# Gated stages of a four-part decoder trunk: weights stationary and tokens moving in units 1 to 10

## The chip, the cores and the metric

The kernel runs on one core of a Trainium2 chip, in one launch. The metric is the device time of one execution in microseconds. All arithmetic is single precision; the projections get it from the faster F32R format by splitting each operand into a high part and a low remainder and adding three products (high x high, high x low, low x high).

## The reference, cut to what matters

256 tokens of 1024 features go through six stages: gated (FF), short convolution, gated, gated, attention, gated. `F` is 2816. Every stage begins with an RMS norm. A gated stage is this:

```python
def rmsnorm(x, g):
    y = x32 * lax.rsqrt(jnp.mean(x32 * x32, axis=-1, keepdims=True) + RMS_EPS)
    return y.astype(x.dtype) * g

def swiglu(x, w_in, w_out):
    gate, up = jnp.split(x @ w_in, 2, axis=-1)      # w_in: 1024 x 5632
    return (jax.nn.silu(gate) * up) @ w_out         # w_out: 2816 x 1024

x = x + 0.5 * swiglu(rmsnorm(x, ln_ff1[i]), w_ff1_in[i], w_ff1_out[i])
```

The norm's factor (one number per token) is not applied to x. The transposed x carries only the gain, and the factor comes in after the projection.

## The kernel before, in words

Every engine has its own hand-written instruction stream; semaphores order them. `t` is one of two tiles of 128 tokens, `s` or `m` the stage, `u` a running count of input weight units, `o` one of output weight units, `c` one of hidden units, `j` the unit within a gated stage (0 to 10). Unit j of a gated stage covers 256 hidden features: 256 gate columns and 256 up columns of `w_in` stand side by side in a 512-column tile, with k = 0 to 7 over the 1024 inputs.

Weights. SP loads `raw_in` (four pieces) and `raw_out` (two halves). ACT copies them to `in_hi`, `out_hi` (`split_in`, `split_out`, lines 414 to 428), DVE subtracts to get `in_lo`, `out_lo` (lines 699 to 711). Both have two slots, used in turn; there is one `raw_in` and one `raw_out`, so SP's next load of a piece waits until DVE has split it.

TensorE. `project` (line 1063) has the transposed activations `xT_hi`, `xT_lo` of 128 tokens as the stationary operand and 512 weight columns as the moving one: 8 k x 3 matmuls for each t, into the bank `proj[t]`, tokens on partitions. ACT applies silu to the gate half of the bank, scaled by the norm factor `rstd` of each partition (`silu`, line 464). DVE multiplies it by the up half and `rstd` (`hidden`, line 766). TensorE transposes the 256 x 256 result in four 128x128 pieces into `tp[0]` (`transpose_hidden`, line 1128), ACT and DVE make `hT_hi` and `hT_lo` of it (lines 469 and 772), and `down_hidden` (line 1094) multiplies it by 256 rows of `w_out` into four `acc` banks that collect over the whole stage: 24 matmuls with 512 moving columns.

Order in a gated stage. `middle(j, par)` on each engine is one turn; TensorE's projects unit j and then does the down matmuls of unit j - 1. Unit 0 is projected first, unit 1 is `middle(1, 1)`, units 2 to 9 run in a loop of four turns with two units each, unit 10 is written out with the last down matmuls, `residual` (line 724: x plus acc times 0.5) and the next stage's norm. The projection of unit 1 waits piece by piece for its weights (`fresh`). An engine's queue is worked off in order, so a wait holds back what stands behind it.

Of the kernel before, what the change touches and what calls it, by code (L numbers as in the profile page):

```python
# [30 lines left out]
ALU = mybir.AluOpType  # L31
# [81 lines left out]
def build(nc, x_in, positions, ln_ff1, w_ff1_in, w_ff1_out, ln_mix, ln_ff2, w_ff2_in, w_ff2_out,  # L113
# [6 lines left out]
    with ExitStack() as ctx:  # L120
# [23 lines left out]
        ident = sb("ident", [P, P])  # L144
        band = sb("band", [P, 2 * P])
# [13 lines left out]
        rstd = sb("rstd", [P, 2 * 7])  # L159
        minus_half = sb("minus_half", [P, 1])  # L160
# [10 lines left out]
        hid_buf = gated[:, W:2 * W].rearrange("p (t n) -> p t n", t=NT)  # L171
        rope_cos = gated[:, 0:W]
# [57 lines left out]
        h_ready = sem("h_ready")  # L230
        hT_ps = sem("hT_ps")
# [133 lines left out]
        def _(pool):  # L365
# [6 lines left out]
            pool.wait_ge(consts_ready, 2)  # L372

# [24 lines left out]
            for m in range(len(STAGES) + 1):  # L398
                for t in range(NT):
# [6 lines left out]
                                       ALU.pow).then_inc(rstd_ready, 1)  # L406
                if m < len(STAGES) and STAGES[m] == ATTN:
                    for n in range(6):
                        rope_sums(n)
# [3 lines left out]
        def _(act):  # L413
# [45 lines left out]
            def silu(c, u, t, first_of=None):  # L459
                act.wait_ge(proj_done, 2 * u + t + 1)  # L460
                if first_of is not None:
                    act.wait_ge(rstd_ready, 2 * first_of + t + 1)
                    act.wait_ge(sq_ready, 2 * first_of + 2)
# [3 lines left out]
            def hidden_hi(c, slot):  # L467
                act.wait_ge(hT_ps, c + 1)
                act.activation(hT_hi[:, slot, :, :].rearrange("p k n -> p (k n)"), tp[0][:, :],  # L469
                               ACT.Copy).then_inc(hT_hi_done, 1)  # L470
# [14 lines left out]
            for s, kind in enumerate(STAGES):  # L485
# [3 lines left out]
                if kind == FF:  # L489
# [4 lines left out]
                    silu(c, u, 0, m)  # L494
                    split_in(u + 1, (u + 1) % 2, (2, 3))
                    silu(c, u, 1, m)
                    split_out(o, o % 2)
                    if s == 0:
# [17 lines left out]
                    silu(c + j, u + j, 0)  # L516
                    hidden_hi(c + j - 1, (c + j - 1) % 2)
                    split_out(o + j, (o + j) % 2)
                    if next_u:
                        split_in(next_u, next_u % 2, (0,))  # L520
                    silu(c + j, u + j, 1)
                    hidden_hi(c + j, (c + j) % 2)
                    if next_u:
                        split_in(next_u, next_u % 2, (1, 2, 3))
# [165 lines left out]
        def _(dve):  # L690
# [33 lines left out]
            def residual(m, t, scale):  # L724

                for half in range(2):
                    if t == 0:
# [5 lines left out]
                    part = x[:, t, half * W:(half + 1) * W]  # L733
                    dve.scalar_tensor_tensor(out=part, in0=acc[t][half][:, :], scalar=scale, in1=part,
# [26 lines left out]
            def hidden(c, t):  # L761

                dve.wait_ge(silu_done, 2 * c + t + 1)
                if not isinstance(c, int) or c >= 1:
                    dve.wait_ge(hT_ps, c)
                dve.scalar_tensor_tensor(out=hid_buf[:, t, :], in0=proj[t][:, UNIT:2 * UNIT],  # L766
                                         scalar=rstd_col[0][:, t:t + 1], in1=silu_buf[:, t, :],
                                         op0=ALU.mult, op1=ALU.mult).then_inc(h_ready, 1)

            def hidden_lo(c, slot):  # L770
                dve.wait_ge(hT_hi_done, c + 1)
                dve.tensor_tensor(hT_lo[:, slot, :, :].rearrange("p k n -> p (k n)"), tp[0][:, :],  # L772
                                  hT_hi[:, slot, :, :].rearrange("p k n -> p (k n)").bitcast(F32),
# [35 lines left out]
            for s, kind in enumerate(STAGES):  # L809
# [3 lines left out]
                if kind == FF:  # L813
                    c = NJ * FF_INDEX[s]
                    split_in(u + 1, (u + 1) % 2, (0, 1))
                    hidden(c, 0)
                    split_in(u + 1, (u + 1) % 2, (2, 3))
                    hidden(c, 1)
# [17 lines left out]
                    hidden(c + j, 0)  # L836
                    hidden_lo(c + j - 1, (c + j - 1) % 2)
                    split_out(o + j, (o + j) % 2)
                    if next_u:
                        split_in(next_u, next_u % 2, (0,))  # L840
                    hidden(c + j, 1)
                    hidden_lo(c + j, (c + j) % 2)
                    if next_u:
                        split_in(next_u, next_u % 2, (1, 2, 3))
# [557 lines left out]
```

## Time and profile before

| what | value |
|---|---|
| median of 3 runs | 956.91 us (955.53 to 957.76) |
| span of the profiled execution | 952.5 us |
| TensorE busy | 937.7 us, 98% |
| DVE, ACT busy | 542.6 us (57%), 440.6 us (46%) |
| weight loads (PEld) recorded | 774.3 us, 4363 of them |
| read from HBM | 167.31 MB, 177 GB/s over the span |

The page does not give the profiled execution a time of its own beside the span; the median of the runs is 4.4 us above the span. PE is the row of matmuls, PEld that of the loads of stationary operands, which overlap the matmuls. A matmul's recorded length (0.39 us) is longer than the distance to the next one's start, because matmuls are pipelined; throughput is read from starts. The granted clock is TensorE's share of its full 2.4 GHz.

### The profile page before, as it was taken

How to read it: one execution, taken by the hardware profiler on the slowest of the kernel's cores; microseconds unless marked ns; L12 is line 12 of the kernel's file. 1: busy time of each engine (PE TensorE's matmuls, PEld its weight loads, DVE VectorE, ACT ScalarE, POOL GpSimd, SP SyncE). 2: the span in 40 equal slices, each digit the busy share in tenths (PEclk: the TensorE clock that was granted, in tenths of full speed). 3: DMA queues.
4: the chain of work that ended last, by engine and by line, in shares of the span. 5: the costliest groups of instructions: out<-in, count | busy, mean ns of one | idle time of the engine just before them, and what ended most of it. 6: DMA issues, size and time to landing. Idle time of an engine off the chain costs nothing.

```text
span 952.5 us, 12737 instructions
## 1 busy us (share of the span) xinstructions
PE 937.7 (98%) x4363; PEld 774.3 (81%) x4363; DVE 542.6 (57%) x646; ACT 440.6 (46%) x615; POOL 28.2 (3%) x55
## 2 busy tenths in 40 slices
PE   7999999999999999999999999999999999999997
PEld 6888888888888888888888888888778888888885
DVE  5754554568656545545575454556866574554534
ACT  6553444456435534444354443534565473444432
POOL 1000000000000000000000000000411000000000
PEclk9999999999999999999999999999999999999999
DMA  8756474447644664656456566563440196465631
GB/s 277 255 186 212 147 223 158 155 154 266 221 146 156 189 216 150 213 166 201 145 197 205 180 198 199 162 218 106 156 154 16 48 318 215 151 215 164 199 109 44
DMA packets 122100, 168.81 MB, mean 177 GB/s; under 512 B 8589, under 2 KB 98773, under 8 KB 122069
## 3 DMA queue, kind: packets, MB, share of 16 engines
q1 hardware_dynamic: 121936, 168.35, 54.7%
q8 instruction: 20, 0.33, 0.1%
q14 instruction: 12, 0.09, 0.0%
q10 hardware_dynamic: 132, 0.04, 0.0%
HBM read 167.31 MB, written 1.05 MB: 177 GB/s over the span
## 4 chain that ended last, share of the span: by engine, by line
PE 94%; DVE 1%; DMA 1%; ACT 1%; POOL 1%; issue 1%; SPq 0%; ACTq 0%; DVEq 0%; POOLq 0%
PE acc L1090 30%; PE proj L1074 19%; PE proj L1076 19%; PE proj L1075 19%; PE tp L1134 2%; PE tp L1125 1%; PE tp L1140 1%; DMA raw_in<-in_w_ff_in 1%; PE proj L1272 1%; PE acc L1272 1%; POOL scratch L395 1%; PE acc L1298 1%; PE tp L1298 1%; DVE in_lo L703 0%; ACT gated L457 0%
## 5 line engine op out<-in xcount | busy, mean ns | idle before, releaser
L1074 PE MATMUL proj<-in_hi,xT_hi 128*128 128x512 f32 x848 | 336.9, 397 | 1.0 <-DVE xT_lo L758 0.6
L1076 PE MATMUL proj<-in_hi,xT_lo 128*128 128x512 f32 x848 | 331.4, 391 | 0.0
L1075 PE MATMUL proj<-in_lo,xT_hi 128*128 128x512 f32 x848 | 330.9, 390 | 0.0
L703 DVE TENSOR_TENSOR in_lo<-raw_in,in_hi 128x1024 fp32r<-128x1024 f32 x212 | 251.0, 1224 | 43.5 <-ACT in_hi L420 43.3
L420 ACT ACTIVATE in_hi<-raw_in 128x1024 fp32r<-128x1024 f32 x212 | 212.7, 1051 | 15.7 <-PE proj L1076 6.2
L464 ACT ACTIVATE gated<-proj,rstd 128x256 f32<-128x256 f32 x88 | 41.6, 473 | 363.7 <-PE proj L1076 363.7
L766 DVE SCALAR_TENSOR_TENSOR gated<-proj,rstd,gated 128x256 f32<-128x256 f32 x88 | 42.6, 484 | 274.5 <-ACT gated L464 274.3
L1074 PEld LDWEIGHTS proj<-in_hi,xT_hi 128*128 128x128 f32 x848 | 159.6, 188 | 35.2 <-issue 1.3
L1076 PEld LDWEIGHTS proj<-in_hi,xT_lo 128*128 128x128 f32 x848 | 159.6, 188 | 34.2
L1075 PEld LDWEIGHTS proj<-in_lo,xT_hi 128*128 128x128 f32 x848 | 159.9, 189 | 31.6
L710 DVE TENSOR_TENSOR out_lo<-raw_out,out_hi 128x1024 fp32r<-128x1024 f32 x96 | 114.2, 1230 | 6.1 <-ACT out_hi L428 6.1
L1090 PE MATMUL acc<-out_lo,hT_hi 128*128 128x512 f32 x352 | 110.1, 390 | 0.0
L1090 PE MATMUL acc<-out_hi,hT_hi 128*128 128x512 f32 x352 | 110.0, 390 | 0.0
L1090 PE MATMUL acc<-out_hi,hT_lo 128*128 128x512 f32 x352 | 109.1, 389 | 0.0
L428 ACT ACTIVATE out_hi<-raw_out 128x1024 fp32r<-128x1024 f32 x96 | 96.1, 1051 | 0.5 <-DMA raw_out<-in_conv_w_out 0.5
L1090 PEld LDWEIGHTS acc<-out_hi,hT_lo 128*128 128x128 f32 x352 | 66.1, 188 | 13.8
L1090 PEld LDWEIGHTS acc<-out_hi,hT_hi 128*128 128x128 f32 x352 | 66.1, 188 | 13.7
L1090 PEld LDWEIGHTS acc<-out_lo,hT_hi 128*128 128x128 f32 x352 | 65.8, 188 | 13.4
L772 DVE TENSOR_TENSOR hT_lo<-tp,hT_hi 128x512 fp32r<-128x512 f32 x44 | 30.4, 692 | 10.5 <-ACT hT_hi L469 7.6
L445 ACT ACTIVATE xT_hi<-pair 128x512 fp32r<-128x512 f32 x24 | 14.8, 633 | 46.8 <-DVE pair L749 46.8
L469 ACT ACTIVATE hT_hi<-tp 128x512 fp32r<-128x512 f32 x44 | 26.3, 598 | 7.1 <-PE tp L1134 7.1
L402 POOL TENSOR_SCALAR mean_sq<-sq_sum 128x1 f32<-128x1 f32 x14 | 2.7, 190 | 884.6 <-ACT gated L457 884.6
(102 smaller groups left out, 468.4 us busy)
## 6 DMA issues: line engine op xcount, KB each, us to landing
raw_in<-in_w_ff_in SPq DMA_DIRECT2D x352, 256.0 KB
raw_out<-in_w_ff_out SPq DMA_DIRECT2D x88, 512.0 KB, 5.4
raw_in<-in_conv_w_in SPq DMA_DIRECT2D x24, 512.0 KB
raw_in<-in_attn_w_qkv SPq DMA_DIRECT2D x12, 512.0 KB
raw_out<-in_conv_w_out SPq DMA_DIRECT2D x8, 512.0 KB, 5.4
raw_out<-in_attn_w_o SPq DMA_DIRECT2D x8, 512.0 KB, 3.3
x<-in_x SPq DMA_DIRECT2D x2, 512.0 KB, 4.6
scratch<-in_ln_final SPq DMA_DIRECT2D x1, 512.0 KB, 4.2
```

The source lines that it names most:

```text
L420: act.activation(in_hi[:, slot, 2 * q:2 * q + 2, :], raw_in[:, 2 * q:2 * q + 2, :], ACT.Copy).then_inc(in_hi_done, 1)
L428: act.activation(out_hi[:, slot, h, :], raw_out[:, h, :], ACT.Copy).then_inc(out_hi_done, 1)
L464: act.activation(silu_buf[:, t, :], proj[t][:, 0:UNIT], ACT.Silu, scale=rstd_col[0][:, t:t + 1]).then_inc(silu_done, 1)
L469: act.activation(hT_hi[:, slot, :, :].rearrange("p k n -> p (k n)"), tp[0][:, :], ACT.Copy).then_inc(hT_hi_done, 1)
L703: dve.tensor_tensor(in_lo[:, slot, 2 * q:2 * q + 2, :], raw_in[:, 2 * q:2 * q + 2, :], in_hi[:, slot, 2 * q:2 * q + 2, :].bitcast(F32), AL ...
L710: dve.tensor_tensor(out_lo[:, slot, h, :], raw_out[:, h, :], out_hi[:, slot, h, :].bitcast(F32), ALU.subtract).then_inc(out_lo_done, 1)
L766: dve.scalar_tensor_tensor(out=hid_buf[:, t, :], in0=proj[t][:, UNIT:2 * UNIT], scalar=rstd_col[0][:, t:t + 1], in1=silu_buf[:, t, :], op0 ...
L772: dve.tensor_tensor(hT_lo[:, slot, :, :].rearrange("p k n -> p (k n)"), tp[0][:, :], hT_hi[:, slot, :, :].rearrange("p k n -> p (k n)").bi ...
L1074: pe.matmul(proj[t][:, :], x_hi, in_hi[:, slot, k, :], start=(k == 0), stop=False)
L1075: pe.matmul(proj[t][:, :], x_hi, in_lo[:, slot, k, :], start=False, stop=False)
L1076: last = pe.matmul(proj[t][:, :], x_lo, in_hi[:, slot, k, :], start=False, stop=(k == KD - 1))
L1090: last = pe.matmul(acc[t][half][:, :], a, part, start=(start and n == 0), stop=(stop and n == 2))
```

## The change

In gated stages, units 1 to 10 exchange the operands of the projection. A 128-column block of the weights is the stationary operand and all 256 tokens are the moving one, so features stand on partitions and tokens along the row. `proj[0]` then holds the gate (two blocks of 256 tokens), `proj[1]` the up part. The product of silu and up is already in the form that the down matmuls take as `hT`, so units 1 to 10 have no transposes. Since the norm factor now varies along the row, it is made into a row: DVE scales the identity by `rstd` for each t, TensorE multiplies a matrix of ones by these diagonals, DVE copies the result, twice side by side, to `rstd_row`. DVE multiplies the gate by this row, ACT applies silu, DVE multiplies by the up part without the factor. Unit 0 keeps its old form but leaves the factor out of its up part too, and `residual` multiplies by `half_rstd` (0.5 times the factor, from POOL) where 0.5 stood. The diff, cut:

```diff
+            def project_f(u, slot, which, cs=(0, 1), fresh=False):
+                if not fresh:
+                    pe.wait_ge(in_lo_done, PIECES * (u + 1))
+                for c in cs:
+                    cols_of = slice((2 * which + c) * P, (2 * which + c + 1) * P)
+                    to = proj[which][:, c * SEQ:(c + 1) * SEQ]
+                    for k in range(KD):
+                        if fresh and c == 0 and k % 2 == 0:
+                            pe.wait_ge(in_lo_done, PIECES * u + k // 2 + 1)
+                        w_hi, w_lo = (a[:, slot, k, cols_of] for a in (in_hi, in_lo))
+                        pe.matmul(to, w_hi, xT_hi[:, k, :], start=(k == 0), stop=False)
+                        pe.matmul(to, w_hi, xT_lo[:, k, :], start=False, stop=False)
+                        last = pe.matmul(to, w_lo, xT_hi[:, k, :], start=False, stop=(k == KD - 1))
+                if 1 in cs:
+                    last.then_inc(proj_done, 1)
+            def row_of_rstd(f):
+                pe.wait_ge(diag_ready, 2 * f + 2)
+                for t in range(NT):
+                    last = pe.matmul(tp[1][:, t * P:(t + 1) * P], ones[:, :], rstd_diag[:, t * P:(t + 1) * P],
+                                     start=True, stop=True)
+                last.then_inc(rstd_row_ps, 1)
 # TensorE, stage body
-                    middle(1, 1, start=True)
+                    def middle(j, par):
+                        pe.wait_ge(gate_scaled, n0 + j)
+                        project_f(u + j, (u + par) % 2, 0)
+                        pe.wait_ge(hid_f_ready, n0 + j)
+                        project_f(u + j, (u + par) % 2, 1)
+                        down_before(j, par)
+                    pe.wait_ge(h_ready, 2 * f + 1)
+                    project_f(u + 1, (u + 1) % 2, 0, (0,), fresh=True)
+                    transpose_hidden(f, c)
+                    row_of_rstd(f)
+                    project_f(u + 1, (u + 1) % 2, 0, (1,))
+                    project_f(u + 1, (u + 1) % 2, 1)
+                    down_before(1, 1, start=True)
 # DVE
                     split_out(o, o % 2)
+                    rstd_to_row(f, m)
+                    hidden_lo(c, c % 2)
                     def middle(j, par):
-                        hidden(c + j, 0)
-                        hidden_lo(c + j - 1, (c + par + 1) % 2)
-                        split_in(u + j + 1, (u + par + 1) % 2, (0, 1, 2))
-                        hidden(c + j, 1)
-                        split_in(u + j + 1, (u + par + 1) % 2, (3,))
+                        split_in(u + j + 1, (u + par + 1) % 2, range(PIECES))
                         split_out(o + j, (o + par) % 2)
+                        gate_f_scaled(u + j, n0 + j)
+                        hidden_f(u + j, n0 + j)
+                        hidden_f_lo(c + j, (c + par) % 2)
+            def rstd_to_row(f, m):
+                for t in range(NT):
+                    dve.tensor_scalar(rstd_diag[:, t * P:(t + 1) * P], ident[:, :], rstd[:, 2 * m + t:2 * m + t + 1],
+                                      None, ALU.mult).then_inc(diag_ready, 1)
+                dve.wait_ge(rstd_row_ps, f + 1)
+                dve.tensor_copy(rstd_row.rearrange("p (k n) -> p k n", k=2),
+                                tp[1][:, 0:SEQ].unsqueeze(1).to_broadcast([P, 2, SEQ])).then_inc(rstd_row_ready, 1)
+            def gate_f_scaled(u, n):
+                dve.wait_ge(proj_done, 2 * u + 1)
+                dve.tensor_tensor(gate_f, proj[0][:, :], rstd_row, ALU.mult).then_inc(gate_scaled, 1)
+            def hidden_f(u, n):
+                dve.wait_ge(proj_done, 2 * u + 2)
+                dve.wait_ge(silu_f_done, n + 1)
+                dve.tensor_tensor(hid_f, proj[1][:, :], gate_f, ALU.mult).then_inc(hid_f_ready, 1)
 # ACT
                     def middle(j, par):
-                        silu(c + j, u + j, 0)
-                        hidden_hi(c + j - 1, (c + par + 1) % 2)
-                        split_in(u + j + 1, (u + par + 1) % 2, (0, 1, 2))
-                        silu(c + j, u + j, 1)
-                        split_in(u + j + 1, (u + par + 1) % 2, (3,))
+                        split_in(u + j + 1, (u + par + 1) % 2, range(PIECES))
                         split_out(o + j, (o + par) % 2)
+                        silu_f(n0 + j)
+                        hidden_f_hi(n0 + j, (c + par) % 2)
```

In unit 10 the order is the same on ACT and DVE with the next stage's first two pieces ahead of the silu and its last two behind the hidden value, and TensorE does 16 of the down matmuls of unit 9 before it waits for unit 10's hidden value.

## Rows read from the trace of the kernel before

**Rows 1.** The page: TensorE's busy time, share, instructions; the last chain, by engine.

```profile
PE 937.7 (98%) x4363; PEld 774.3 (81%) x4363; DVE 542.6 (57%) x646; ACT 440.6 (46%) x615; POOL 28.2 (3%) x55
...
PE 94%; DVE 1%; DMA 1%; ACT 1%; POOL 1%; issue 1%; SPq 0%; ACTq 0%; DVEq 0%; POOLq 0%
```

**Rows 2.** One middle unit, all engines; the first line names the columns.

```profile
core 0: us, PE busy (x) PEld busy (x) DVE busy (x) ACT busy (x) POOL busy (x), PEclk, DMA share, GB/s
307.48:324.29 16.81, 16.81 (x77) 13.91 (x76) 8.65 (x9) 7.20 (x9) 0.00 (x0) 1.00 0.77 244
```

**Rows 3.** The chain in order of time: start us, length us, what.

```profile
34.38 5.44 PE acc L1090 x24
```

**Rows 4.** TensorE around the transposes, by time: start us, length us, line.

```profile
307.25 0.39 PE L1076 MATMUL proj<-in_hi,xT_lo 128*128 128x512 f32 x1
307.49 0.60 PE L1134 MATMUL tp<-ident,gated 128*128 128x128 f32 x4
307.84 0.48 PE L1074 MATMUL proj<-in_hi,xT_hi 128*128 128x512 f32 x1
308.15 0.40 PE L1075 MATMUL proj<-in_lo,xT_hi 128*128 128x512 f32 x1
308.39 0.40 PE L1076 MATMUL proj<-in_hi,xT_lo 128*128 128x512 f32 x1
...
310.47 0.39 PE L1076 MATMUL proj<-in_hi,xT_lo 128*128 128x512 f32 x1
```

**Rows 5.** Weight loads in order of time, same stretch.

```profile
307.81 0.19 PEld L1074 LDWEIGHTS proj<-in_hi,xT_hi 128*128 128x128 f32 x1
307.92 0.19 PEld L1075 LDWEIGHTS proj<-in_lo,xT_hi 128*128 128x128 f32 x1
```

**Rows 6.** Weight loads of 64-column matmuls; each row begins with a start.

```profile
702.64 0.30 PEld L1298 LDWEIGHTS acc<-scratch 128*128 128x128 f32 x2
...
702.75 0.30 PEld L1298 LDWEIGHTS acc<-scratch 128*128 128x128 f32 x2
```

**Rows 7.** TensorE at the lower clock: one window, then two starts.

```profile
684.10:687.30 3.20, 3.20 (x10) 2.52 (x9) 3.04 (x4) 2.49 (x3) 1.38 (x2) 0.50 0.01 3
...
685.46 0.63 PE L1074 MATMUL proj<-in_hi,xT_hi 128*128 128x512 f32 x1
685.89 0.63 PE L1075 MATMUL proj<-in_lo,xT_hi 128*128 128x512 f32 x1
```

**Rows 8.** Score matmuls, 256 columns; each row begins with a start.

```profile
700.30 0.59 PE L1272 MATMUL acc<-scratch 64*128 64x256 f32 x2
...
700.51 0.59 PE L1272 MATMUL acc<-scratch 64*128 64x256 f32 x2
...
700.73 0.38 PE L1272 MATMUL acc<-scratch 64*128 64x256 f32 x1
```

**Rows 9.** Second gated stage: TensorE, ACT, DVE after unit 0's projection.

```profile
302.04 0.39 PE L1074 MATMUL proj<-in_hi,xT_hi 128*128 128x512 f32 x1
...
302.24 0.47 ACT L464 ACTIVATE gated<-proj,rstd 128x256 f32<-128x256 f32 x1 [1.49 <-PE proj L1076]
...
302.75 0.48 DVE L766 SCALAR_TENSOR_TENSOR gated<-proj,rstd,gated 128x256 f32<-128x256 f32 x1
303.70 2.36 DVE L710 TENSOR_TENSOR out_lo<-raw_out,out_hi 128x1024 fp32r<-128x1024 f32 x2 [0.47 <-ACT out_hi L428]
```

**Rows 10.** The last gated stage at the same place.

```profile
771.08 0.50 PE L1074 MATMUL proj<-in_hi,xT_hi 128*128 128x512 f32 x1
...
772.63 1.22 DVE L703 TENSOR_TENSOR in_lo<-raw_in,in_hi 128x1024 fp32r<-128x1024 f32 x1
...
774.16 2.35 DVE L710 TENSOR_TENSOR out_lo<-raw_out,out_hi 128x1024 fp32r<-128x1024 f32 x2
```

**Rows 11.** Groups by line: busy us, mean ns of one, idle time before.

```profile
L772 DVE TENSOR_TENSOR hT_lo<-tp,hT_hi 128x512 fp32r<-128x512 f32 x44 | 30.4, 692 | 10.5 <-ACT hT_hi L469 7.6
...
L866 DVE TENSOR_SCALAR scratch<-scratch,cols 128x256 f32<-128x256 f32 x8 | 2.3, 349 | 1.4 <-ACT scratch L540 1.4
```

More of the change, by code:

```diff
@@ L144, in build @@
         ident = sb("ident", [P, P])
+        ones = sb("ones", [P, P])
         band = sb("band", [P, 2 * P])
@@ L171, in build @@
         hid_buf = gated[:, W:2 * W].rearrange("p (t n) -> p t n", t=NT)
+        gate_f, hid_f = gated[:, 0:W], gated[:, W:2 * W]
+        rstd_row = pair[:, 0, :]
+        rstd_diag = pair[:, 1, 0:SEQ]
         rope_cos = gated[:, 0:W]
@@ L230, in build @@
         h_ready = sem("h_ready")
+        half_ready = sem("half_ready")
+        diag_ready = sem("diag_ready")
+        rstd_row_ps = sem("rstd_row_ps")
+        rstd_row_ready = sem("rstd_row_ready")
+        gate_scaled = sem("gate_scaled")
+        silu_f_done = sem("silu_f_done")
+        hid_f_ready = sem("hid_f_ready")
         hT_ps = sem("hT_ps")
@@ L372, in _ @@
             pool.wait_ge(consts_ready, 2)
+            pool.memset(ones[:, :], 1.0).then_inc(ident_ready, 1)
             pool.affine_select(out=band[:, :], in_=band[:, :], compare_op=ALU.is_ge, fill=NEG, base=-1,
@@ L406, in _ @@
                                        ALU.pow).then_inc(rstd_ready, 1)
+                    if m < len(STAGES) and STAGES[m] == FF:
+                        pool.wait_ge(rstd_ready, i + 1)
+                        pool.tensor_scalar(half_rstd[:, i:i + 1], rstd[:, i:i + 1], 0.5, None,
+                                           ALU.mult).then_inc(half_ready, 1)
                 if m < len(STAGES) and STAGES[m] == ATTN:
@@ L493, in _ @@
                     split_in(u + 1, (u + 1) % 2, (0, 1))
-                    silu(c, u, 0, m)
+                    silu(u, 0, m)
                     split_in(u + 1, (u + 1) % 2, (2, 3))
-                    silu(c, u, 1, m)
+                    silu(u, 1, m)
                     split_out(o, o % 2)
+                    f = FF_INDEX[s]
+                    n0 = (NJ - 1) * f - 1
+                    hidden_hi(f, c % 2)
                     if s == 0:
@@ L722, in split_late_out, with residual @@
                                       ALU.subtract).then_inc(out_lo_done, 1)
-            def residual(m, t, scale):
+            def residual(m, t):
                 for half in range(2):
+                    if t == 0 and half == 0 and STAGES[m - 1] == FF:
+                        dve.wait_ge(half_ready, 2 * (FF_INDEX[m - 1] + 1))
                     if t == 0:
@@ L733, in residual @@
                     part = x[:, t, half * W:(half + 1) * W]
+                    i = 2 * (m - 1) + t
+                    scale = half_rstd[:, i:i + 1] if STAGES[m - 1] == FF else 1.0
                     dve.scalar_tensor_tensor(out=part, in0=acc[t][half][:, :], scalar=scale, in1=part,
@@ L759, in norm_rest, with hidden @@
                                       xT_hi[:, ks, ts].bitcast(F32), ALU.subtract).then_inc(xT_lo_done, 1)
[L761 to L768, printed above, removed]
+            def hidden(f, t):
+                dve.wait_ge(silu_done, 2 * f + t + 1)
+                if f >= 1:
+                    dve.wait_ge(hT_ps, f)
+                dve.tensor_tensor(hid_buf[:, t, :], proj[t][:, UNIT:2 * UNIT], silu_buf[:, t, :],
+                                  ALU.mult).then_inc(h_ready, 1)
             def hidden_lo(c, slot):
@@ L1046, in _ @@
                 for t in range(NT):
-                    residual(m + 1, t, 0.5 if kind == FF else 1.0)
+                    residual(m + 1, t)
                     if s + 1 < len(STAGES):
@@ L1163, in _, with down_before @@
                     c = NJ * FF_INDEX[s]
-                    def middle(j, par, start=False):
-                        for t in range(NT):
-                            pe.wait_ge(h_ready, 2 * (c + j - 1) + t + 1)
-                            project(m, u + j, t, (u + par) % 2, fresh=(start and t == 0))
-                            if t == 0:
-                                transpose_hidden(c + j - 1)
+                    f = FF_INDEX[s]
+                    n0 = (NJ - 1) * f - 1
+                    def down_before(j, par, start=False):
                         pe.wait_ge(hT_lo_done, c + j)
@@ L1183, in _ @@
                     j = NJ - 1
-                    for t in range(NT):
-                        pe.wait_ge(h_ready, 2 * (c + j - 1) + t + 1)
-                        project(m, u + j, t, (u + j) % 2)
-                        if t == 0:
-                            transpose_hidden(c + j - 1)
+                    pe.wait_ge(gate_scaled, n0 + j)
+                    project_f(u + j, (u + j) % 2, 0)
+                    pe.wait_ge(hid_f_ready, n0 + j)
+                    project_f(u + j, (u + j) % 2, 1)
                     pe.wait_ge(hT_lo_done, c + j)
@@ L1192, in _ @@
                     slots = ((c + j - 1) % 2, (o + j - 1) % 2)
-                    down_hidden(*before, 0, *slots, parts=range(0, 4))
-                    transpose_hidden(c + j)
-                    down_hidden(*before, 0, *slots, parts=range(4, 6))
+                    down_hidden(*before, 0, *slots)
                     down_hidden(*before, 1, *slots, parts=range(0, 2))
```

60 lines of the change are left out of this document (36 added, 24 removed).

## Prediction

> **What bounds the kernel now.** I read the page first, then the windows of single units, then single starts on TensorE. The page shows TensorE busy for 98% of the span, and the chain of waits that ended last lies on it for 94% [rows 1]. So the time is a count of matmuls times the distance between their starts. One middle unit of a gated stage takes 16.81 us; TensorE fills all of it at the full granted clock (1.00, which is 2.4 GHz), while DVE works 8.65 us and ACT 7.20 us in it and the DMA engines are 0.77 busy [rows 2]. Nothing but TensorE ends a wait there. Its 24 matmuls of the down projection take 5.44 us, 0.2267 us each [rows 3]. A unit has 48 + 24 such matmuls, 16.32 us; the other 0.49 us of 16.81 belong to the four transposes. They are seen in the starts: last matmul before them at 307.25, transposes from 307.49, the second matmul after them at 308.15, and the ten distances from there to 310.47 mean 0.232 us and not 0.227 [rows 4].
>
> The number that decides is not in a busy share: how long TensorE needs from start to start when the moving operand is 256 columns and every matmul has a new stationary tile. Loads and streams overlap: a load begins just as the matmul before it does, and in a run of 512 columns it is out of sight [rows 4, 5].
>
> **The change, part by part.**
>
> *1. The projections of units 1 to 10.* Out go 48 matmuls of 512 columns per unit, in come 96 of 256 columns (two outputs, two column blocks, eight k, three products). The columns streamed are the same, the weight loads double. There are 40 such units. The bounds of one 256-column distance:
> - A load occupies its port for about 0.11 us: two loads after a pause start at 307.81 and 307.92 [rows 5], and in a run of 64-column matmuls the loads set the beat at 0.11 us (702.64, 702.75) [rows 6]. So 0.112 us is the floor, an estimate from these starts.
> - The stream: 512 columns at 2.4 GHz are 0.2133 us, the measured distance is 0.2267, so 0.0133 us are lost per matmul. If the loss goes with the columns, 256 cost 0.1133 us. If it goes with the load or with the instruction, they cost 0.1067 + 0.0133 = 0.120 us.
> - Which? At the lower granted clock (0.50, 1.2 GHz) the distance is 0.427 us, exactly 512 columns with nothing lost [rows 7]. So the loss is not a fixed count of array cycles; it is something on the supply side that does not show when the array is slow. The plain F32 score matmuls, 256 columns streamed twice, stand 0.21 and 0.22 us apart [rows 8], again with nearly nothing lost, though each has a load. And after a pause the distance wanders (0.23 to 0.24 us) before it settles [rows 4]. A loss that depends on how load and stream stand to each other looks like the two disturbing each other, and then each load costs it. In the new loop a load runs beside almost all of each stream, so I take 0.120 us. The widest distance there, 0.24 us from 308.15 to 308.39, is a loss of 0.0267 us and bounds it above: 0.1067 + 0.0267 = 0.133 us. Below: 0.112.
> Sum: 96 x 0.120 + 24 x 0.2267 = 11.52 + 5.44 = 16.96 us per unit without transposes, against 16.81 with them: +0.15 us, times 40 = **+6 us**. At the ends of the range: 0.112 gives 16.19, -0.62 us, -25 us in all; 0.133 gives 18.21, +1.40 us, +56 us in all. Each 0.001 us in this distance is 3.8 us in the result.
>
> *2. The transposes.* Eleven groups of four per stage become one (unit 0 keeps its own). That is the 0.49 us of each of 40 units, 19.6 us, and it is already inside the +6 (the projections alone cost +25.6).
>
> *3. The norm factor as a row, once per stage.* DVE scales two 128x128 diagonals (some 0.25 us each, an estimate from 349 ns for 128x256 [rows 11]), TensorE multiplies them by ones (two plain F32 matmuls, which the kernel's others show as two records each, so four at the load's 0.11 us), DVE copies the row. TensorE's part of it is about 0.45 us, and 0.1 us for the load that shows after a wait. But the diagonals stand on DVE behind the two splits of the down weights, and TensorE waits for them in order, with 72 projection matmuls queued behind. In the stage at 302 us unit 0's last projection ends at 302.04; silu follows at 302.24, the hidden product at 302.75, the splits of the down weights on DVE run from 303.70 to 306.06 [rows 9]. The diagonals would be ready at about 306.6. TensorE has 24 short matmuls (2.9 us) and the transposes (0.44 us) to fill the time: it is there at 305.4 and waits 1.3 us. In the stage at 771 us (and in the first stage, which is built and fed alike) the weights of unit 1 arrive late: TensorE starts at 771.08, the last piece of unit 1 is split at 773.85, the down weights at 776.51 [rows 10]. Now the first half covers 2.9 us and not 5.4: about 0.55 us of waiting for the last piece, transposes until 775.1, diagonals at 777.1, 2.0 us of waiting. Sum: 2 x 1.3 + 2 x 2.55 + 4 x 0.6 = **+10 us**. This could be nothing if the splits came later than the diagonals, which the order forbids; at worst the splits wait for a transfer, another 1 us per stage.
>
> *4. DVE and ACT in a middle unit.* DVE loses two products of 0.48 us [rows 9] and one of 692 ns and gets three 512-column operations of about 692 ns [rows 11]: 8.65 - 1.66 + 2.07 = 9.1 us of some 17. ACT stays at about 7 us. The splits now run in one block from the end of a unit's projections: some 2.5 us for the hidden value, then 6 pieces at 1.22 us on DVE, over about 10 us later, and the gate of the next unit is ready 11 us later. What waits behind it: the product with the row must be done before TensorE needs that bank again, some 10 us later. Cost nothing; the cover is the 5.4 us of down matmuls and 5.8 us of the other half of the projection, and each microsecond beyond it would be 40 in the result. SP's loads follow the same splits, which come in one block and have about 9 us to land. At a share of 0.77 [rows 2] the bytes of a unit keep the DMA engines 12.9 us busy, so they fit in 17 us; cost nothing, with the same 40 for each microsecond of lateness.
>
> *5. Small edits, one answer.* The residual takes its factor from a column that POOL made a stage earlier, and hidden rows leave one factor out: same instruction, no cost. The extra fill of ones is done on POOL before x has arrived. At a stage's end the last hidden value is ready 2.4 us after its projection, and 16 down matmuls (3.6 us) cover that, where four transposes stood before.
>
> **The sum.** Span 952.5 + 6 + 10 = 968.5 us. The median of the runs, 956.9, is 4.4 above the profiled span; with the same 4.4 the forecast is 973 us.
>
> **The rivals.**
> - *A, the loss goes with the columns or vanishes (faster).* The distance is then 0.112 to 0.1145 us. At 0.1133 the projections cost what they did, the transposes give 19.6 back, the boundaries take 10: 947 us. For it: rows 8, where streams with loads lose nearly nothing. Against: rows 4, where the distance changes with the same columns. It decides below 0.1158 us, where 3840 x 0.0025 equals the 9.6 us that are left.
> The Trainium skill has a rule that ends on this side: "TensorE: Matmul & The Clock Gate", Back-to-back issue gap, gives columns / 2.4 + 2.5 ns for a warm stream, 109 ns for 256 columns; worked out from the page, an estimate, the sum is 931 us. For 512 columns it gives 216 ns, and the trace has 227 [rows 3]; the measurement decides.
> - *B, nearly even.* 0.1145 to 0.117 us: 952 to 961 us.
> - *C, load and stream disturb each other more when both last 0.107 us.* 0.124 to 0.133 us: 988 to 1023 us. For it: every stream is now under a load from end to end. Against: a steady run settles at the smallest loss [rows 4].
> - *D, loads don't hide.* Each load is recorded with 0.19 us [rows 5]. If that were its real occupancy, 96 x 0.188 + 5.44 = 23.5 us per unit, +267 us, some 1235 us. Against: loads that start 0.11 us apart [rows 5, 6].
> A page speaks for D: "Perfetto Trace Analysis" in the Trainium skill, Identifying the Most-Contended Engine, takes the busy share of LDWEIGHTS as the measure of TensorE's headroom; it is 13.91 of 16.81 us here [rows 2], and the change adds 48 loads to 76.
>
> **How the numbers follow.** The forecast (0.117 to 0.124 us, 961 to 988 us): 0.51. A: 0.22. B: 0.07. C: 0.16. D: 0.04. About 0.2% is what a measurement of this kernel can tell from no change. Faster: A and a little of B, 0.24; same, 955 to 959: 0.04; slower 0.72. The range reaches from A's 944 to 1004 us (0.128), in the middle of C; it leaves out D, the upper half of C and the lowest edge of A. The likeliest case's own range is 961 to 988.
>
> **What would show it.** In the changed profile: the down matmuls still 0.2267 us apart; the new projection matmuls in a steady run 0.120 apart (0.113 says A, over 0.124 says C, 0.19 or more D); a unit of 16.96 us; TensorE idle 1.3 to 2.6 us once per gated stage, ended by DVE's diagonal; no idle time in the loops. The prediction is wrong if the distance is off by more than 0.003 us, or if the loops show waits for DVE, ACT or a transfer.

## The result, and the profile after

| | before | after |
|---|---|---|
| median of the runs | 956.2 us (955.5 to 957.8, 4 runs) | 972.65 us (970.2 to 975.3, 4 runs) |
| span of the profiled execution | 952.5 us | 970.3 us |
| TensorE matmul records | 4363 | 6139 |

The change makes the kernel slower: the ratio is 1.0181, with a 95% interval of 1.0162 to 1.0200. The forecast was 973. One execution of ten of the kernel "High and low x side by side" below took 1559 us at a mean granted clock of 0.557 and is left out of its numbers; all others in this document had 0.98 or more.

The page of the changed kernel, busy time by engine and the chain by engine, beside [rows 1]:

```profile
PE 948.5 (98%) x6139; PEld 860.9 (89%) x6139; DVE 559.5 (58%) x658; ACT 436.3 (45%) x575; POOL 34.5 (4%) x64
...
PE 90%; DVE 3%; DMA 2%; ACT 2%; POOL 1%; issue 1%; SPq 1%; DVEq 0%; POOLq 0%; ACTq 0%
```

TensorE is as full as before, and the weight loads rise from 81% to 89% busy. The chain leaves TensorE more often than before (90% and not 94%).

One middle unit, from the end of one block of down matmuls to the end of the next, beside [rows 2]:

```profile
core 0: us, PE busy (x) PEld busy (x) DVE busy (x) ACT busy (x) POOL busy (x), PEclk, DMA share, GB/s
326.74:343.72 16.98, 16.98 (x122) 16.02 (x122) 9.88 (x11) 7.79 (x9) 0.00 (x0) 1.00 0.58 194
```

And the same unit's neighbours in the chain in order of time (start us, length us, what), beside [rows 3]:

```profile
321.27 5.47 PE acc L1147 x24
338.25 5.47 PE acc L1147 x24
```

A unit takes 338.25 - 321.27 = 16.98 us, where it was 16.81; TensorE still has no gap in it. (In the kernel before the units alternate between 16.81 and 16.79 us, so their mean is 16.80; the changed kernel's are all 16.98.) The new projection matmuls, TensorE by time:

```profile
350.03 0.28 PE L1197 MATMUL proj<-xT_hi,in_hi 128*128 128x256 f32 x1
350.15 0.28 PE L1198 MATMUL proj<-xT_lo,in_hi 128*128 128x256 f32 x1
350.27 0.28 PE L1199 MATMUL proj<-xT_hi,in_lo 128*128 128x256 f32 x1
```

Each row's length (0.28 us) is how long one matmul is in the engine; what it costs is the distance to the next start, 0.12 us.

The second gated stage at its boundary, all engines by time, to be read against [rows 9]:

```profile
308.17 0.42 DVE L795 TENSOR_TENSOR gated<-proj,gated 128x256 f32<-128x256 f32 x1 [0.18 <-ACT gated L480]
...
309.12 2.36 DVE L735 TENSOR_TENSOR out_lo<-raw_out,out_hi 128x1024 fp32r<-128x1024 f32 x2 [0.52 <-ACT out_hi L445]
...
310.34 0.60 PE L1217 MATMUL tp<-ident,gated 128*128 128x128 f32 x4
...
311.40 0.48 DVE L807 TENSOR_SCALAR pair<-ident,rstd 128x128 f32<-128x128 f32 x2
...
311.93 0.71 PE L1207 MATMUL tp<-pair,ones 128*128 128x128 f32 x4 [0.99 <-DVE pair L807]
312.39 0.36 PE L1197 MATMUL proj<-xT_hi,in_hi 128*128 128x256 f32 x1
```

DVE's hidden product and splits are at 308.17 and 309.12, TensorE's transposes at 310.34, and TensorE then waits for the two diagonals, which DVE makes behind the splits of the down weights. Over the whole kernel, the waits of the weight loads:

```profile
PEld tp L1207 <- DVE pair L807: 6.1, 4, 1.8
```

Four waits, one in each gated stage, 6.1 us in all. Where the 17.8 us of span went can be read from the transposes of x that open each stage; in the chain of the changed kernel those of five stages are

```profile
199.31 0.87 PE tp L1182 x8
...
292.21 0.87 PE tp L1182 x8
...
482.28 0.87 PE tp L1182 x8
...
672.35 0.87 PE tp L1182 x8
...
768.91 0.88 PE tp L1182 x8
```

and in the chain of the kernel before they stand at

```profile
194.25 0.87 PE tp L1125 x8
...
286.79 0.87 PE tp L1125 x8
...
473.45 0.87 PE tp L1125 x8
...
660.10 0.87 PE tp L1125 x8
...
755.61 0.87 PE tp L1125 x8
```

So the first gated stage takes 199.31 - 194.25 = 5.1 us more than before, the convolution stage 0.4, the second and third gated stage 3.4 each, the attention stage 1.1, and the last gated stage (to the end of the span) 4.5. In the convolution and attention stages TensorE has the same matmuls in every kernel of this document, and yet they take 92.5 to 93.0 us and 93.9 to 97.3 us in its ten traces. So their 0.4 and 1.1 us are within what varies from trace to trace, and the change itself costs the 16.4 us of the four gated stages, which is also the difference of the two medians.

### The profile page after: what moved, and what is told of

Its sections match the earlier page's. It is cut to its first block, busy times and chain, and to the rows that moved or that the text cites. A ratio compares the mean times of both kernels' runs of the same rounds, so it can differ in the third digit from the quotient of the medians.

```text
span 970.3 us, 16110 instructions
## 1 busy us (share of the span) xinstructions
PE 948.5 (98%) x6139; PEld 860.9 (89%) x6139; DVE 559.5 (58%) x658; ACT 436.3 (45%) x575; POOL 34.5 (4%) x64
## 4 chain that ended last, share of the span: by engine, by line
PE 90%; DVE 3%; DMA 2%; ACT 2%; POOL 1%; issue 1%; SPq 1%; DVEq 0%; POOLq 0%; ACTq 0%
PE acc L1147 28%; PE proj L1199 15%; PE proj L1198 15%; PE proj L1197 15%; PE proj L1131 4%; PE proj L1133 4%; PE proj L1132 4%; DMA raw_in<-in_w_ff_in 1%; DVE out_lo L735 1%; PE tp L1223 1%; PE tp L1182 1%; DVE in_lo L728 1%; PE proj L1363 1%; PE acc L1363 1%; POOL scratch L408 1%
## 5 line engine op out<-in xcount | busy, mean ns | idle before, releaser
L1197 PE MATMUL proj<-xT_hi,in_hi 128*128 128x256 f32 x1280 | 363.0, 284 | 1.3 <-DVE gated L795 0.9
L1199 PE MATMUL proj<-xT_hi,in_lo 128*128 128x256 f32 x1280 | 362.2, 283 | 0.0
L1198 PE MATMUL proj<-xT_lo,in_hi 128*128 128x256 f32 x1280 | 362.2, 283 | 0.0
L1197 PEld LDWEIGHTS proj<-xT_hi,in_hi 128*128 128x128 f32 x1280 | 245.5, 192 | 4.4 <-DVE gated L795 1.7
L1198 PEld LDWEIGHTS proj<-xT_lo,in_hi 128*128 128x128 f32 x1280 | 245.6, 192 | 1.5
L1199 PEld LDWEIGHTS proj<-xT_hi,in_lo 128*128 128x128 f32 x1280 | 245.5, 192 | 0.0
L823 DVE TENSOR_TENSOR gated<-proj,gated 128x512 f32<-128x512 f32 x40 | 27.7, 692 | 184.4 <-PE proj L1199 181.3
L735 DVE TENSOR_TENSOR out_lo<-raw_out,out_hi 128x1024 fp32r<-128x1024 f32 x96 | 113.1, 1219 | 24.4 <-ACT out_hi L445 24.4
L1131 PE MATMUL proj<-in_hi,xT_hi 128*128 128x512 f32 x208 | 83.6, 402 | 1.0 <-DVE xT_lo L787 1.0
L1133 PE MATMUL proj<-in_hi,xT_lo 128*128 128x512 f32 x208 | 81.5, 392 | 0.0
L1132 PE MATMUL proj<-in_lo,xT_hi 128*128 128x512 f32 x208 | 81.5, 392 | 0.0
```

Source lines behind the costliest of these rows:

```text
L735: dve.tensor_tensor(out_lo[:, slot, h, :], raw_out[:, h, :], out_hi[:, slot, h, :].bitcast(F32), ALU.subtract).then_inc(out_lo_done, 1)
L823: dve.tensor_tensor(hid_f, proj[1][:, :], gate_f, ALU.mult).then_inc(hid_f_ready, 1)
L1131: pe.matmul(proj[t][:, :], x_hi, in_hi[:, slot, k, :], start=(k == 0), stop=False)
L1132: pe.matmul(proj[t][:, :], x_hi, in_lo[:, slot, k, :], start=False, stop=False)
L1133: last = pe.matmul(proj[t][:, :], x_lo, in_hi[:, slot, k, :], start=False, stop=(k == KD - 1))
L1197: pe.matmul(to, w_hi, xT_hi[:, k, :], start=(k == 0), stop=False)
```

## The experiments

**Diagonals first.** The changed kernel, with the two diagonals made by DVE ahead of the splits of the down weights.

```diff
                     hidden(f, 1)
+                    rstd_diagonals(f, m)
                     split_out(o, o % 2)
                     rstd_to_row(f, m)
```

> The changed kernel, with the two diagonal scalings on DVE moved ahead of the two splits of the down weights (the copy of the row stays behind them). Theory: TensorE's four waits for the diagonal (1.85, 1.27, 1.27 and 1.85 us from the last transpose to the next record, 5.8 us over the usual distance) vanish and nothing is late next, because the copy of the row is needed only 10 us later: 5.8 us less than the changed kernel, about 966.8 us. Rival: unit 1's hidden value or its weights are late next and the wait only moves: under 1 us gained, 972 us.

Measured: 963.5 us (962.9 to 966.3, 4 runs), ratio to the kernel before 1.0081 (1.0057 to 1.0106). The changed kernel's ratio is 1.0181, so this one edit gives back about 1.0% of the time by the medians, 0.6% by the profiled spans (970.3 - 964.5 = 5.8 us; the gated stages alone are 6.2 us shorter). The forecast of this run was 966.8; the profiled execution, 966.3 us, was the slowest of the four and the other three took about 963. Where those 3 us come from isn't shown. TensorE around the boundary of the second gated stage, by time:

```profile
308.08 0.60 PE L1221 MATMUL tp<-ident,gated 128*128 128x128 f32 x4
308.51 0.61 PE L1211 MATMUL tp<-pair,ones 128*128 128x128 f32 x4
308.88 0.36 PE L1201 MATMUL proj<-xT_hi,in_hi 128*128 128x256 f32 x1
```

The row of the norm factor follows the transposes at once. From transposes to next projection it is 0.80 us and not 2.05 (312.39 - 310.34). The order on DVE was the cause of the wait, and no other work of DVE took its place here. One new gap of 0.6 us is in this trace, at 41 us, before unit 2 of the first stage, and ends with DVE's gate product; the last kernel below is without it.

**The kernel before with 256 columns.** Only the length is changed: tokens stay stationary, each projection of units 1 to 10 is done in two blocks of 256 weight columns, the transposes stay.

```diff
+                wide = W // parts
+                for part in range(parts):
+                    cs = slice(part * wide, (part + 1) * wide)
...
-                    pe.matmul(proj[t][:, :], x_hi, in_hi[:, slot, k, :], start=(k == 0), stop=False)
+                        pe.matmul(proj[t][:, cs], x_hi, in_hi[:, slot, k, cs], start=(k == 0), stop=False)
```

> The kernel before, in which only the projections of units 1 to 10 of each gated stage are cut into two column halves: same operands and roles, tokens stationary, 96 matmuls of 256 columns where 48 of 512 stood; transposes and all waits as before. Theory (the loss of 13.3 ns is paid per matmul, whatever its operands): distance 0.120 us, 1920 more matmuls x 0.0133 = +25.6 us over the kernel before, about 982 us. Rival (the loss goes with the exchange of roles, for example because weights that DVE has just written are now loaded as stationary tiles): distance 0.1133 us, no change, 956 us.

Measured: 977.9 us (977.5 to 979.8), ratio 1.0241 (1.0214 to 1.0268), span 975.6. A window of one unit, with the columns of [rows 2], and TensorE by time:

```profile
353.29:370.70 17.41, 17.41 (x126) 16.45 (x125) 8.65 (x10) 7.19 (x10) 0.00 (x0) 1.00 0.57 182
```

```profile
350.09 0.28 PE L1078 MATMUL proj<-in_lo,xT_hi 128*128 128x256 f32 x1
350.21 0.28 PE L1079 MATMUL proj<-in_hi,xT_lo 128*128 128x256 f32 x1
```

The distance is 0.12 us with the other operand stationary and other data. It belongs to the length, not to the exchange of the operands. The unit is 17.41 us, 0.60 over the kernel before; the changed kernel's is 16.98, and the 0.43 us between them are the transposes.

The time is 4 us under the 982 that was expected. The units give 24.4 us and not 25.6, since the 0.06 us that the transposes disturb behind them in the kernel before are not there at 256 columns (96 x 0.120 + 24 down matmuls in 5.47 + four transposes in 0.43 are 17.42 us). The attention stage is 1.6 us shorter in this trace (93.9 and not 95.5 us): it has no stretch at the lower clock, where the kernel before has 3.4 us of it.

**The transposes twice.** The kernel before, with each group of four transposes of the hidden value done two times over.

```diff
-                for kt in range(2):
+                for kt in (0, 1, 0, 1):
```

> The kernel before, with each group of four transposes of the hidden value done twice into the same places. Theory: TensorE has no slack, so 44 groups x 4 x 0.108 us = +19.1 us, about 975 us. Together with the unit's 16.81 us this gives the price of a group, 0.49 us, of which 0.06 us stay with the change of pattern. Rival: part of the transposes runs in time that TensorE has anyway: less than +12 us.

Measured: 973.65 us (973.0 to 975.4), ratio 1.0194 (1.0167 to 1.0221), span 971.6, +19.1 in span. The down matmuls of two units in a row in its chain:

```profile
34.81 5.44 PE acc L1090 x24
52.06 5.44 PE acc L1090 x24
```

The unit is 17.25 us here, +0.44 (17.23 and +0.43 in the mean of two). That is the difference between the last two kernels again, to 0.01: the second group costs the bare four transposes, and the 0.06 us of disturbed matmuls behind a group come once. Of the 19.1 us 0.8 are the attention stage's (last section); the gated stages' 18.4, over the 44 groups of the kernel, are 0.42 each.

**The vector engine does more.** The changed kernel, with DVE's product for the hidden value done once more into a buffer that nobody reads.

```diff
+                dve.tensor_tensor(rstd_twin, proj[1][:, :], gate_f, ALU.mult)
                 dve.tensor_tensor(hid_f, proj[1][:, :], gate_f, ALU.mult).then_inc(hid_f_ready, 1)
```

> The changed kernel, with the product of the up part and the activated gate made once more on the vector engine, into a buffer that nobody reads: 0.69 us more on that engine in each of 40 units, just ahead of the hidden value that the down projection waits for. Theory (there is slack of several us behind the 48 products of the other half): no change, ratio to the changed kernel 0.999 to 1.001, so about 972.5 us. Rival (the vector engine's chain is already close to the limit in a unit): up to 40 x 0.69 = 28 us more, 1000 us.

Measured: 970.8 us (970.6 to 971.7, 4 runs), ratio to the kernel before 1.0161 (1.0142 to 1.0180), so not slower than the changed kernel. Its chain:

```profile
37.74 5.47 PE acc L1149 x24
54.72 5.47 PE acc L1149 x24
```

A unit stays at 16.98 us. 40 x 0.68 = 27 us more work on DVE costs nothing; DVE is no bound in the changed loop.

**Half the stationary columns.** The kernel before, with 64 of the 128 token columns as stationary operand in the projections of units 1 to 10; half the tokens' projection is left out there. It asks where the 0.0133 us beyond the stream come from.

```diff
-                    x_hi, x_lo = (a[:, k, t * P:(t + 1) * P] for a in (xT_hi, xT_lo))
+                    x_hi, x_lo = (a[:, k, t * P:t * P + rows_of] for a in (xT_hi, xT_lo))
```

> The kernel before, with only 64 of the 128 token columns of the stationary operand in the projections of units 1 to 10; the projection of half the tokens is left out there. 48 x 40 matmuls of 512 columns keep their stream and get a load of half as many columns. Theory 1 (the 13.3 ns over the stream are what the array needs between two matmuls, whatever is loaded): distance 0.2267 us as before, time unchanged, ratio 0.998 to 1.002. Theory 2 (the load takes something from the stream while it runs, in proportion to its size): distance 0.220 us, 1920 x 0.0067 = 13 us less, about 942 us, ratio 0.986. Theory 3 (the loss is in the number of rows that a matmul writes): the same 0.220 us, which this run does not tell from theory 2.

Measured: 962.1 us (959.8 to 963.4), ratio 1.0073 (1.0054 to 1.0092), a unit of 16.95 us: no theory expected slower. Loads by form, then starts on TensorE by time:

```profile
L1075 PEld LDWEIGHTS proj<-in_lo,xT_hi 128*64 128x64 f32 x640 | 86.2, 135 | 56.3
...
L1075 PEld LDWEIGHTS proj<-in_lo,xT_hi 128*128 128x128 f32 x208 | 39.1, 188 | 7.5
```

```profile
357.09 0.40 PE L1075 MATMUL proj<-in_lo,xT_hi 128*64 128x512 f32 x1
357.33 0.39 PE L1076 MATMUL proj<-in_hi,xT_lo 128*64 128x512 f32 x1
...
359.17 0.39 PE L1075 MATMUL proj<-in_lo,xT_hi 128*64 128x512 f32 x1
```

The load is recorded shorter (135 ns and not 188), but the distance grows: nine distances from 357.09 to 359.17 mean 0.231 us and not 0.227, and they vary from row to row. So the loss is not in proportion to the size of the load. Beyond that its cause stays open.

**128 columns.** The kernel before with four blocks of 128 columns, the edit as above with `parts=4`.

> The kernel before, with the projections of units 1 to 10 cut into four blocks of 128 columns: 192 matmuls with their weight loads per unit in place of 48, the same columns and the same products. A stream of 128 columns takes 0.053 us, so the load is the longer of the two. Theory (a load occupies its port for about 0.11 us and hides all else): distance 0.107 to 0.112 us, unit 192 x 0.11 + 5.44 + 0.49 = 27.0 us, +10.2 us x 40, about 1365 us. Rival 1 (the 13 ns come on top of the longer of the two): 0.122 us, unit 29.4 us, about 1455 us. Rival 2 (13 ns on top of the stream, loads always hidden): 0.067 us, about 1020 us.

Measured: 1393 us (one execution), span 1391.4. TensorE by time, a pair of units in the chain, and a window near the start with its granted clock:

```profile
129.99 0.28 PE L1077 MATMUL proj<-in_hi,xT_hi 128*128 128x128 f32 x1
130.10 0.27 PE L1078 MATMUL proj<-in_lo,xT_hi 128*128 128x128 f32 x1
130.21 0.28 PE L1079 MATMUL proj<-in_hi,xT_lo 128*128 128x128 f32 x1
```

```profile
119.68 5.50 PE acc L1093 x24
146.98 5.50 PE acc L1093 x24
```

```profile
26.00:66.00 40.00, 40.00 (x183) 39.42 (x183) 10.87 (x22) 7.07 (x12) 0.00 (x0) 0.50 0.29 93
```

The distance is 0.11 us, where the stream alone would be 0.053: with 128 columns the load sets the beat, as forecast from [rows 5, 6]. The unit is 27.3 us, 40 x 10.5 = 420 us of the 439 us of span. The first gated stage takes 20 us more than that, and they are in the window: from 26 to 66 us the granted clock was 0.50 (1.2 GHz); there the short matmuls stand 0.213 us apart. They began at 22.65 us, and TensorE paused twice before the clock fell: ahead of 24.34 and of 25.47 us, the second time for 0.25 us for a piece of the weights. I had not foreseen that, and one execution doesn't show its cause.

**High and low x side by side.** "Diagonals first", and then the one use of the exchange that makes instructions longer: the high part of the weights is multiplied by [high x | low x], 512 columns, and the low part by high x, 256 columns into the second half of the same bank; DVE adds the halves. That is 32 + 32 matmuls per unit in place of 96.

```diff
-                        pe.matmul(to, w_hi, xT_hi[:, k, :], start=(k == 0), stop=False)
-                        pe.matmul(to, w_hi, xT_lo[:, k, :], start=False, stop=False)
-                        last = pe.matmul(to, w_lo, xT_hi[:, k, :], start=False, stop=(k == KD - 1))
+                        pe.matmul(both, in_hi[:, slot, k, cols_of], xT[:, :, k, :], start=(k == 0), stop=False)
+                    for k in range(KD):
+                        last = pe.matmul(to[:, SEQ:2 * SEQ], in_lo[:, slot, k, cols_of], xT_hi[:, k, :],
+                                         start=False, stop=(k == KD - 1))
```

> The kernel with early diagonals, in which the two products that share a weight tile (high weights by high x and by low x) become one matmul of 512 columns, high x and low x side by side, and the low weights' product adds into the second half; the two halves are added by DVE (ten more 256-column operations in the place of two of 512, less two), and the up part uses the two tp banks. Theory (a fixed 13.3 ns per matmul): per block and k 0.2267 + 0.120 = 0.3467 us in the place of 0.360, 32 of them per unit: 0.43 us less per unit, 17 us less than the kernel with early diagonals: about 950 us, 6 below the kernel before. Rival: the mixture of lengths never settles (5 ns more per 512-column matmul, 6 us) or the longer DVE chain (about 1.7 us more from the end of a projection to the hidden value) shows at the stage ends, 1 us each: 956 to 960 us.

Measured: 953.6 us (951.7 to 955.8), ratio 0.9981 (0.9965 to 0.9997), span 951.8. Its chain, and its waits on TensorE:

```profile
54.41 5.47 PE acc L1163 x24
71.03 5.47 PE acc L1163 x24
```

```profile
PE proj L1213 <- DVE in_lo L730: 1.9, 4, 0.6
PE proj L1213 <- DVE gated L827: 1.2, 1, 1.2
```

The unit is down to 16.62 us, where 16.55 (0.43 less than 16.98) had been expected: 40 x 0.19 = 7.6 us won in the loop against the kernel before. Most of it went into waits outside it: for late pieces in the first units (line 730), and 1.2 us at 41 us for the gate, which DVE makes behind the rotary angles in the first stage.

**The same, with those waits cured.** Unit 1 takes the wide and the narrow product of each k in turn, all others 16 wide and then 16 narrow ones; the rotary angles come after unit 1's hidden value.

```diff
-                    for k in range(KD):
-                        if fresh and c == 0 and k % 2 == 0:
...
+                if fresh:
+                    for k in range(KD):
...
+                        wide(0, k)
+                        last = narrow(0, k)
```

> The kernel of the run before with 512-column products for the high weights, cured of the waits that its trace showed: in the first half of unit 1 the 512-column product and the 256-column product of one k follow each other, so that a late piece of the weights blocks less; in all other units both column blocks of a half run their 16 wide products first and then their 16 narrow ones, so that the length changes once and not twice per half; the angles of the rotary table are computed after unit 1's hidden value and not before it. Theory (TensorE's starts alone set the time): the wait of 1.58 us at 41 us goes, the waits for late pieces shrink from 3.5 us in all to about 2.3, and half of the changes of length go, 80 times some 0.02 us. Span 951.8 - 1.6 - 1.2 - 1.6 = 947.4 us, time about 949, ratio to the kernel before 0.993 to 0.994. Rival (the late pieces are set by the transfers, the angles then delay the loop instead): 952 to 954 us, ratio 0.997 to 1.000.

Measured: 950.5 us (948.5 to 951.8, 6 runs), ratio 0.9942 (0.9926 to 0.9958), span 950.0. The waits and the chain:

```profile
PE proj L1211 <- DVE gated L797: 0.6, 1, 0.6
```

```profile
52.16 5.47 PE acc L1163 x24
68.73 5.47 PE acc L1163 x24
```

The wait for the gate at 41 us is gone (line 827 no longer stands among TensorE's waits), the late pieces cost 0.3 us and not 1.9, and the unit is 16.57 us. The three edits were made together, so what each gave was not taken apart. This kernel beats both: 0.6% faster than the one before, 2.3% faster than the changed one (950.5 / 972.65). By the spans it is 2.5 us under the kernel before; its gated stages alone are 4.8 us shorter, and its attention stage, 1.8 us longer in this trace, hides the rest.

## Why the prediction was right

The forecast was right in its time and, nearly everywhere, in its working. Two errors of about 2 us nearly cancel: the span is 970.3 and not 968.5 us, and the median is 2.3 and not 4.4 us above it. They are largely one error. Each execution on record takes 1.8 to 1.9 us longer than its own span, so some 2.5 of the 4.4 us were only that the profiled execution of the kernel before was quicker than its median one. From median to median the forecast added 16 us, and 16.4 were measured. That it hit 973 to 0.4 us is luck all the same: the four executions of the changed kernel lie 5 us apart.

- *Step 1, the distance.* 0.120 us was taken of bounds 0.112 to 0.133, and 0.120 it is, in both kernels that were tried with 256 columns. The choice between "the loss goes with the columns" and "the loss goes with the instruction" carried the sign of the answer; A's 0.1133 would have made the change a gain. The unit is 16.98 us and not 16.96, since the 24 down matmuls take 5.47 us and not 5.44: the first few behind a change of length are up to 0.01 us late. That is +7 us in 40 units where 6 were forecast. The reason given, that load and stream disturb each other, is not shown: the loss is there once per matmul, but half a load did not lower it. Every projection matmul in these kernels has a load of its own, so no run tells a loss per load from a loss per instruction. The plain F32 score matmuls of [rows 8] show nearly none of it, and no run asked why. So the distance was right, and its reason stays open.
  What hangs on rival A's page follows: by the rule in the Trainium skill, "TensorE: Matmul & The Clock Gate", Back-to-back issue gap, 256 columns would stand 109 ns apart; the trace has 120 ns, and 227 for 512 columns where the rule gives 216. The section gives this rule for the gap of a single matmul, without a budget for loads, which the prediction did not say. The measurement decides.
- *Step 2, the transposes.* 0.49 us was taken; the two pairs of kernels give 0.43 us for the four transposes themselves, and 0.06 for what they disturb behind them. It was already inside the unit.
- *Step 3, the boundaries.* In the middle stages 10 x 0.15 + 1.3 + 0.6 = 3.4 us was forecast, and both measured 3.4. In detail: the wait is 1.2 us and not 1.3, the ten units 1.8 and not 1.5, and 0.4 us and not 0.6 are left for the rest. The waits in the first and the last stage are 1.8 us and not 2.0. In the first and the last stage 4.65 us was forecast and 5.1 and 4.5 measured. "Diagonals first" shows that it is this wait: without it the span is 5.8 us shorter, where 2 x 1.3 + 2 x 2.0 = 6.6 had been put down for the diagonals. What then stays at each boundary beside the units (row matmuls, late pieces) is 0.4 us in the middle stages, 0.9 in the last and 1.3 in the first, 0.6 of it the new gap at 41 us.
- *Step 4, the other engines.* No cost, and none found: the units show no gap, and 0.69 us more of DVE in each changed nothing. DVE was put at 9.1 us, and the nine instructions of a unit add up to that: 3 x 0.69 for the products and the low part, 4.63 for the splits of four pieces, 2.35 for those of two halves, 9.05 in all. The window shows 9.88 because a part of the next unit's instructions falls into it. The gate's product of that unit starts at 332.53, and TensorE takes its bank again at 343.56, 10.3 us after the product has ended.
- *Step 5, small edits.* The end of a stage shows 36 down matmuls in a row and the transposes of x behind them: nothing waits for the last hidden value there.
- *Not forecast.* The convolution stage takes 0.4 us more and the attention stage 1.1, which were put at nothing; these 1.5 us are most of the error in the span, and they vary as much between traces of other kernels. That the offset of one execution to the median carries over was an assumption, and it was off by 2 us.
- *Rival D* falls: the loads are recorded with 0.19 us and stand 0.12 apart, with 89% of the span busy. By the Trainium skill, "Perfetto Trace Analysis", Identifying the Most-Contended Engine, TensorE's headroom is judged by the busy share of LDWEIGHTS, together with the share of peak FLOPs that is used; by the share of the loads alone, as the prediction took it, [rows 2] leaves 2.9 us of 16.81, room for 15 loads of 0.19 us, and the trace has 44 more in a unit that grew by 0.17 us. The overlap of the records decides here, not their share.

## What to carry to other kernels

Cost a matmul by the distance of starts at its own moving length, from the trace: here, at 512 and at 256 columns, a fixed 0.013 us sits on each F32R matmul with its load beside 0.1067 us per 256 columns. So twice the instructions for the same columns cost 24 us in 40 units, more than the 17 us that the saved transposes gave. If an exchange of the operands puts two products on the same stationary tile, join them into one long stream, which is where the gain was. And ahead of a serial step that TensorE waits for, look at what stands in front of it on its engine: two 0.28 us scalings behind two 1.2 us splits cost 6 us.

## What the runs showed that had not been expected

- A projection matmul whose stationary operand has 64 columns and not 128 is no cheaper: 0.231 us against 0.227 us for the same 512 streamed columns, though its load is recorded with 135 ns and not 188.
- With 128-column streams the granted clock was 0.50 from 26 to 66 us and then 1.00 to near the end, with TensorE busy in all of the stretch at 0.50. In the other nine traces the stretches at 0.50 lasted about 3 to 7 us. All nine have one at the end, and seven have one in the attention stage, behind TensorE's wait there. The kernel before with 256 columns and the one with half the stationary columns have none there, though TensorE waited for as long (2.2 and 3.2 us); why is not shown.
- The wait of TensorE for POOL in the attention stage has two values, whatever the gated stages do: 2.2 us in five of the traces (the kernel before and the changed one with more DVE work among them), 3.2 us in the five others (the changed one among them). POOL's last sum before it and DVE's split beside it, by time, in the changed kernel:

```profile
691.06 5.41 DVE L728 TENSOR_TENSOR in_lo<-raw_in,in_hi 128x1024 fp32r<-128x1024 f32 x4
...
695.35 1.43 POOL L409 TENSOR_TENSOR scratch<-gated 128x128 f32<-128x128 f32 x1
```

and in the kernel before:

```profile
683.11 0.45 POOL L396 TENSOR_TENSOR scratch<-gated 128x128 f32<-128x128 f32 x1
...
683.33 1.31 DVE L703 TENSOR_TENSOR in_lo<-raw_in,in_hi 128x1024 fp32r<-128x1024 f32 x1 [0.50 <-ACT in_hi L420]
```

The same sum takes 1.43 us when it starts beside a running split of DVE, and 0.45 us when it starts in DVE's pause of 0.50 us. So 1 us of the changed kernel's attention stage hangs on when a piece of the weights was ready; the changed kernel with more DVE work, which waits 2.2 us there, takes 95.54 us for that stage, and the kernel before 95.51. DVE's splits are longer there too, 5.41 us for four against 4.63 in the loop. That the two engines hinder each other is read from these rows; no run took the splits away. The Trainium skill, "SBUF — State Buffer", Who interferes with whom, says that a VectorE instruction with two inputs in SBUF contends with a GpSimd instruction that reads SBUF, since the two engines share a pair of ports that is an exclusive lock. The splits have two such inputs, and the rows agree with it: the sum's 0.98 us of extra time are not more than one split's.
